# Two transformer blocks in one kernel: when rows are turned before the gate's product, in which order its pairs of tiles are taken, and where the last product's seven-multiplication steps sit

## The reference, cut to what matters

```
x = x + (silu(gate) * up) @ w_ffn_out          # hidden width 5632
ple = p @ w_ple
x = x + sigmoid(rmsnorm(x, ple_norm_g) @ w_ple_gate) * ple
...
u = causal_dwconv(h @ w_up, ffn_conv_w) + ffn_conv_b
x = x + (silu(gate) * val) @ w_down            # hidden width 5632, the last product
return rmsnorm(x, g_final)
```

## Time and profile before

| | us |
|---|---|
| median of 3 runs | 2427.86 (2427.65 to 2429.02) |
| the profiled execution's own time | 2427.8 |
| its span in the trace | 2426.0 |
| TensorE busy | 2408.2 (99%) |
| DVE busy | 1622.3 (67%) |
| ACT busy | 1310.8 (54%) |
| DMA, mean | 225 GB/s |

### The profile page before, as it was taken

How to read it: one execution, slowest core, us unless ns; L and a number is a source line. 1 busy time by engine, 2 the same in 40 slices (tenths; PEclk the granted TensorE clock), 3 DMA queues, 4 the chain that set the end, 5 groups by cost and what they waited for, 6 DMA issues and landing times.

```text
span 2426.0 us, 27837 instructions
## 1 busy us (share of the span) xinstructions
PE 2408.2 (99%) x10666; PEld 1994.6 (82%) x10666; DVE 1622.3 (67%) x2009; ACT 1310.8 (54%) x1608; POOL 189.4 (8%) x349
## 2 busy tenths in 40 slices
PE   9999999999999999999999999999999999999998
PEld 8888888888888888888887888888888888887887
DVE  7575555667555555569786864786567766778886
ACT  7555566445444444445455654545566666665554
POOL 0000000001000000000001010110111110110000
PEclk9999999999999999999999999999999999999999
DMA  8777665778767677676668777887888878886664
GB/s 278 224 223 225 196 197 176 226 228 254 220 211 229 210 219 220 211 220 205 202 208 274 233 240 219 252 246 236 235 246 245 243 244 240 242 242 202 219 203 159
DMA packets 155014, 545.85 MB, mean 225 GB/s; under 512 B 20097, under 2 KB 20609, under 8 KB 154625
## 3 DMA queue, kind: packets, MB, share of 16 engines
q1 hardware_dynamic: 131120, 470.91, 61.7%
q0 software_dynamic: 23184, 72.37, 10.9%
q10 hardware_dynamic: 576, 0.79, 0.1%
HBM read 505.72 MB, written 38.27 MB: 224 GB/s over the span
## 4 chain that ended last, share of the span: by engine, by line
PE 97%; DVE 2%; ACT 1%; DMA 0%; issue 0%; SPq 0%; ACTq 0%; DVEq 0%
PE ps L1782 96%; DVE wl L1239 1%; ACT wh L891 0%; DMA PR<-in_p 0%; PE ps L1921 0%; DMA XG<-in_x 0%; DVE xs_in L1286 0%; PE ps L1941 0%; DVE tmp L1663 0%; DVE tmp L1670 0%; DVE wl L1275 0%; DVE xs_out L1288 0%; ACT wh L914 0%; ACT tmp L1177 0%; PE ps L1922 0%
## 5 line engine op out<-in xcount | busy, mean ns | idle before, releaser
L1239 DVE TENSOR_TENSOR wl<-raw,wh 128x1024 fp32r<-128x1024 f32 x826 | 1008.0, 1223 | 765.1 <-ACT wh L891 764.0
L891 ACT CAST wh<-raw 128x1024 fp32r<-128x1024 f32 x826 | 864.5, 1049 | 924.5 <-PE ps L1782 919.3
L1782 PE MATMUL ps<-wh,x1g_hi 128*128 128x512 f32 x704 | 273.9, 389 | 0.0
L1782 PE MATMUL ps<-wl,x1g_hi 128*128 128x512 f32 x704 | 273.9, 389 | 0.0
L1782 PE MATMUL ps<-wh,x1g_lo 128*128 128x512 f32 x704 | 273.9, 389 | 0.0
L1782 PE MATMUL ps<-wh,x4g_hi 128*128 128x512 f32 x704 | 273.9, 389 | 0.0
L1782 PE MATMUL ps<-wl,x4g_hi 128*128 128x512 f32 x704 | 273.9, 389 | 0.0
L1782 PE MATMUL ps<-wh,x4g_lo 128*128 128x512 f32 x704 | 273.9, 389 | 0.0
L1782 PE MATMUL ps<-wh,h_hi 128*128 128x512 f32 x576 | 225.0, 393 | 0.8 <-ACT wh L896 0.8
L1782 PE MATMUL ps<-wh,h_lo 128*128 128x512 f32 x576 | 223.4, 390 | 0.0
L1782 PE MATMUL ps<-wl,h_hi 128*128 128x512 f32 x576 | 223.2, 390 | 0.0
(11 more groups left out here) (348 smaller groups left out, 3564.2 us busy)
## 6 DMA issues: line engine op xcount, KB each, us to landing
raw<-in_w_in SPq DMA_DIRECT2D x196, 512.0 KB, 4.3
raw<-in_w_ffn_in SPq DMA_DIRECT2D x176, 512.0 KB, 4.3
raw<-in_w_up SPq DMA_DIRECT2D x176, 512.0 KB, 4.5
raw<-in_w_ffn_out SPq DMA_DIRECT2D x88, 512.0 KB, 3.8
raw<-in_w_down SPq DMA_DIRECT2D x88, 512.0 KB, 4.2
rows<-Y POOLq DMA_DIRECT2D x67, 512.0 KB, 4.8
Z<-rows POOLq DMA_DIRECT2D x268, 128.0 KB, 4.8
raw<-in_w_o SPq DMA_DIRECT2D x32, 512.0 KB, 4.5
```

What stands on the lines that cost most here:

```text
L891: e.copy(wh[:, i % RING, :], raw[:, slot, :]).then_inc(rounded, 1)
L1239: e.tensor_tensor(wl[:, r, :], raw[:, i % RAW, :], wh[:, r, :].bitcast(F32), ALU.subtract).then_inc(remainder, 1)
L1782: return e.matmul(dst, weights, x, start=start, stop=stop, skip_group_check=True)
```

## The change

Four edits, all of the plan. Nothing is computed otherwise.

1. **Turning for the gate.** The four chunks are turned from steps 68, 73, 82 and 91 of out1 on (before 77, 82, 87, 92). `plan_unfold` can place `squares` apart from the turn: for chunks 0 and 1 they stand in step 78 (before: 78 and 83), for chunks 2 and 3 in steps 83 and 92, beside their turns.
2. **Order of the gate's pairs.** The cuts of the first two chunks are (0, 4, 6, 8) in place of (0, 6, 8): four pairs of chunk 0, four of chunk 1, then two, two, two and two.
3. **Sums of activations.** For the last product the three groups begin in steps 5, 9 and 13 in place of 5, 8 and 11. For out1 they stay three steps apart.
4. **Order of the last product's pairs.** The first unit of seven stands at position 10 in place of 9, which is granule 20 in place of 18, and all six units of q = 0 follow one position later. The tail begins at position 21 in place of 20.

```diff
-DOWN_ORDERS = ((0, 1, 2, 3, 4, 5, 6, 7, 9, 8, 11, 10, 13, 12, 15, 14, 17, 16, 19, 18, 20, 21),
+DOWN_ORDERS = ((0, 1, 2, 3, 4, 5, 6, 7, 9, 11, 8, 13, 10, 15, 12, 17, 14, 19, 16, 20, 18, 21),
                (0, 1, 2, 3, 4, 8, 5, 10, 6, 12, 7, 14, 9, 16, 11, 18, 13, 15, 17, 19, 20, 21))
-DOWN_TAILS = (20, 16)
+DOWN_TAILS = (21, 16)
...
-        def plan_unfold(s, stage, n, late, filled):
+        def plan_unfold(s, stage, n, late, filled, squares_at=None):
             s += late
 
             def leave():
-                do("squares", stage, n)
+                if squares_at is None:
+                    do("squares", stage, n)
                 rows_of[stage, n] = turn(s + 1, X[:, :, 512 * n:512 * n + 512], filled)
...
+            if squares_at is not None:
+                later(squares_at, lambda: do("squares", stage, n))
             later(s + 1, leave)
             later(s + 8, take)
...
-        def plan_x_sums(stage, step):
+        def plan_x_sums(stage, step, every):
             for j in range(3):
-                later(step + 3 * j, lambda j=j: do("xs_sum", stage, j))
-                later(step + 3 * j + 1, lambda j=j: do("xs_hi", stage, j))
-                later(step + 3 * j + 2, lambda j=j: do("xs_lo", stage, j))
+                for k, name in enumerate(("xs_sum", "xs_hi", "xs_lo")):
+                    later(step + every * j + k, lambda name=name, j=j: do(name, stage, j))
...
-        plan_x_sums("out1", len(granules) + 4)
+        plan_x_sums("out1", len(granules) + 4, 3)
...
-        for n, step in enumerate((77, 82, 87, 92)):
-            later(out_from + step, lambda s=out_from + step, n=n: plan_unfold(s, "ple", n, 0, ("residual", "ple", n)))
+        for n, step in enumerate((68, 73, 82, 91)):
+            later(out_from + step, lambda s=out_from + step, n=n: plan_unfold(
+                s, "ple", n, 0, ("residual", "ple", n), max(s, out_from + 77) + 1))
...
         product_pair(t["w_ple_gate"], "ple", PAIRS16, [("pgate", 0), ("pgate", 1)],
-                     [plan_one("ple_gate", 0), plan_one("ple_gate", 1)], then=[lambda n=n: ple_product(n) for n in range(2)])
+                     [plan_one("ple_gate", 0), plan_one("ple_gate", 1)], (0, 4, 6, 8), then=[lambda n=n: ple_product(n) for n in range(2)])
...
-        plan_x_sums("down", down_from + 5)
+        plan_x_sums("down", down_from + 5, 4)
```

## The result

The changed kernel takes 2418.19 us (median of 6 runs, 2417.80 to 2419.13), the kernel before 2428.39 beside it (6 runs, 2427.52 to 2429.56). The ratio is 0.9958, 95% interval 0.9947 to 0.9968. It is faster by 10.2 us; 2417.6 us were forecast, and the range and the bound of 0.2% (2423.0 in the prediction) hold. The profiled execution took 2418.17 with a span of 2416.4, where 2426.0 stood before: 9.6 us.

The account below looks back on a forecast made before the run. TensorE was taken as the bound, busy 2408.2 of 2426.0 us, so only its gaps could go: 2427.8 - 7.25 (gate) - 4.39 (last product) + 1.4 (second unit) = 2417.6 us, range 2415.6 to 2422.4.

Parts of the forecast that it names:

- the bound of 0.2%: Whole kernel: 4.9 us, about what a measurement can tell from no change, so faster means below 2423.0 us.
- The gate, 7.25 us: At the gate: edits 1 and 2 remove TensorE's wait for x2g_lo and the clock loss, winning 7.25 us.
- The cover behind mem, 0: Gate granules 97 to 100 behind the mem load: delays stay hidden with 0.8 us to spare; cost 0, bounds 0 and 3.
- the rival: Gate granules 97 to 100: cover behind mem gives way, new wl stall of 1 to 3 us, say 2419.6; chance 0.17.
- The moved turns, 0: Earlier turns of the gate's chunks delay DVE and ACT work, but within cover; cost 0, bounds 0 and 2 us.
- ACT's wait for Z of chunk 0: Step 76: ACT reaches turned_hi at 1263.5 and waits 1.6 us for Z, there at about 1265.
- the slower rival: Step 76: ACT stands for chunk 0's Z, its casts queue behind; 2434.6 us if Z is 20 us late; chance 0.03.
- The last product, 4.39 us gone: Last product: edits 3 and 4 remove three small late starts (1.1 us) and the first unit's stall, 4.39 us together.
- The second unit, 1.4 us back: Last product's second unit: GF's load goes out between its two raw granules, costing 1.4 us; bounds 0 and 3.
- The sum: Whole kernel: 2427.8 - 7.25 - 4.39 + 1.4 = 2417.6 us, also taken for the median; chance 0.45.
- the stated bounds: Costs at the upper end: 3 us at the gate behind mem, 2 us for the moved turns, 3 us at the second unit.
- the first unit's late bound: Last product's first unit: DVE's sums start at 2232.8 instead of 2231.6, so 1 us less is won.

Follow-up runs that it names:

- the kernel with p later: Kernel before, with p_hi and p_lo two steps later (96 and 97); 2427.90 us, ratio 0.9993.
- The second load of mem: Changed kernel with a second 2 MB load of mem right behind the first, first use waiting for both; 2422.36 us, ratio 0.9973.
- Taking GF away: Changed kernel with load_gf moved from step 20 of the last product to step 22 (2416.72 us) or step 44 (2416.70 us).
- the three kernels with the gate mended alone: Kernel before plus edits 1 and 2 (2422.02 us), edit 1 only (2421.71 us), or edit 2 only (2421.32 us).
- the three kernels that lose at most 0.2 us at the two places: Changed kernel with load_gf in step 22 (2416.72 us), in step 44 (2416.70 us), and in step 44 without edit 1 (2416.91 us).

## Why the prediction was right, point by point

- *The gate, 7.25 us.* Right in place and size: the wait, the slow first matmuls and the clock of 0.63 are gone. The step missed how the two edits share it: either alone takes all of it. It also left pp_lo out of the chain (0.6 us on DVE), and said nothing of how often the clock falls; it didn't in the kernel with p later.
- *The cover behind mem, 0.* Right, and to 0.2 us in each of its times: cast 97 at 1322.08 (1321.9), granule 99 at 1331.6 (1331.6), granule 100 at 1334.8 (1334.9). In the first of them there is luck: the raw granule was issued at 1311.9, 0.8 us later than the prediction had it, and landed after 10.1 us in place of 10.8. The second load of mem shows that the rival was 1 us away, not impossible.
- *The moved turns, 0.* Right on DVE and in the casts: `shared_second` ends at 1272.1 (1272.1) and the cast of step 79 starts at 1274.78 (1274.6):

```profile
1263.61 1.70 ACT L1074 ACTIVATE x2g_hi<-Z,cst 128x256 fp32r<-128x256 f32 x4
...
1274.78 1.98 ACT L894 CAST wh<-raw 128x1024 fp32r<-128x1024 f32 x2
```

  Wrong in one step: ACT's wait for Z of chunk 0, forecast 1.6 us, isn't there (first row, ACT of the changed kernel). I had carried the 8.2 us from turn to `bring` over from a later and busier stretch. POOL in the changed kernel:

```profile
1254.82 2.18 POOL L1750 DMA_DIRECT2D Z<-rows  x4 [3.71 <-DMA rows<-Y]
```

  It waited 3.71 us for the rows, before 7.08. The DMA engines were busy for 0.72 of the time there (1250 to 1255), against 0.83 over 1272 to 1277 in the kernel before; that this makes the difference is not shown. The error cost nothing, and it made the slower rival look nearer than it was.
- *The last product, 4.39 us gone.* 4.2 went: what stays beside the second unit is 0.15 us of short starts at the first. The sums at 2224.65 against a forecast of 2231.6 less 7.25, which is 2224.35. The sizes inside were off: the prediction gave edit 3 the 1.1 us of the small starts and edit 4 the rest. Edit 3 is worth 1.9: ACT's wait for the third `xs_sum` costs the 1.1 of the small starts and makes the unit's chain on DVE 1.9 late, of which 0.8 reach TensorE. The sum of the two was not affected.
- *The second unit, 1.4 us back.* Right in mechanism, 1.7 in size. The granule behind GF took 6.5 us in place of 6.3 and was issued 0.3 later than walked. Taking GF away removes this and nothing else. The granule ahead of GF took 3.6 us and the one behind it 6.5, 2.9 more for 1 MB, where the rows of before gave 2.7. The Trainium skill, page DMA: Bandwidth & Descriptors, section Anatomy of one DMA, gives the moving part of a DMA that GpSimd issues as bytes / 436 GB/s, which for 1 MB is an estimate of 2.4. GF is issued by SP, and the measured 2.9 decides. By the skill's rule that each DMA engine takes descriptors in the order of the ring (section Queues, rings and completion order) the granule behind GF is the late one. The trace agrees: 6.5 us behind it, 3.6 ahead of it.
- *The sum.* Forecast 10.24, found 7.25 + 2.52 = 9.77 in the losses, 9.6 in the span; the other 0.2 are lost in the first 30 us of the kernel, which no edit touches. That the median fell by 10.2, so close to the forecast, is luck: it comes from the kernel before, whose medians (2428.39 here, 2428.68 to 2429.17 beside the experiments) lie above its profiled execution of 2427.8. The upper end of the range, 2422.4, doesn't follow from the stated bounds: 3 at the gate and 3 in place of 1.4 at the second unit give 2417.6 + 4.6 = 2422.2, and the 1 us of the first unit's late bound is not in it. The time lies far below either.
- *Adding the places.* The prediction treated gate and last product as independent. By the medians on one chip they are: 7.15 us for edits 1 and 2 and 3.16 for edits 3 and 4 make 10.3, and all four give 10.2. By the profiles they are not: in the three kernels with the gate mended alone the last product lost 1.04 us more, for the clock fell at its gap, and the spans give 5.7 and 1.4. The kernel before was profiled in one of its shorter executions, with a mean granted clock of 0.998, while 13 of its 16 executions on that chip show 0.997. If the clock falls at the last product's gap in most of its executions too, both accounts agree; no profile shows that.

## What to carry to other kernels

When a stage is mended so that it issues its loads sooner, or a granule is moved by a step, look at which unrelated load shares the new step: a load of 1 MB put between two granules that one unit needs cost 1.7 us, and two steps later nothing. Before adding the gains of two edits, ask whether they remove the same wait (edits 1 and 2), and whether one wait has two results, of which only one has been priced (ACT's wait behind edit 3): each was only seen by making each edit alone. And price a gap of the matrix engine with the clock it may lose, even where the one profile at hand doesn't show the loss: here 1.04 us after a wait of 2.3 us.

## What the hardware showed that I had not expected

- The length of a gap doesn't settle whether the clock falls. After the last product's gap it fell in the profiles of three kernels (waits of 2.3 to 2.4 us) and stayed in the kernel before and the one with p later (2.3); after a wait of 3.5 us at the gate it stayed, after 5.1 to 6.3 it fell in every profile. What else decides was not found.
- Without the gaps the times lie closer together: the times of the three kernels that lose at most 0.2 us at the two places (5, 5 and 4 runs) spread over 1.24, 0.55 and 1.45 us, the 18 of the kernel before on the chip of the first two over 3.8. More runs spread wider by themselves, so the numbers don't give the size of the effect.
